# Down products of a macaron encoder layer: affine of tiles 0-3 two steps sooner, statistics of tiles 4-7 by a sum on VectorE and squares on ScalarE

## What is computed

```python
def sublayer(h, j, fn, resid_w):
    u = (_layer_norm(h) * (1.0 + scale) + shift).astype(h.dtype)
    z = DEEPNORM_ALPHA * h.astype(jnp.float32) + resid_w * gate * fn(u)
    return (_layer_norm(z) * ln_g[layer, j] + ln_b[layer, j]).astype(h.dtype)

def _layer_norm(x):
    mu = jnp.mean(xf, axis=-1, keepdims=True)
    var = jnp.mean(jnp.square(xf - mu), axis=-1, keepdims=True)
    return (xf - mu) * lax.rsqrt(var + LN_EPS)

def _swiglu(u, w_gate, w_up, w_down):
    return (jax.nn.silu(u @ w_gate) * (u @ w_up)) @ w_down
```

## Time and profile before

| | |
|---|---|
| time, median of 3 runs | 2078.71 us (2077.89 to 2082.67) |
| profiled execution | 2078.98 us, span 2077.2 us |
| TensorE busy | 1959.9 us (94%) |
| VectorE busy | 1195.8 us (58%) |
| ScalarE busy | 801.3 us (39%) |
| GpSimd busy | 606.4 us (29%) |
| TensorE waits, 1960 us to the end | 2.7 us for VectorE L1465, 2.0 for L1431 (extra), 0.7 for L1431 (4 times) |

### The profile page before, as it was taken

The page is one execution under the profiler, slowest core; times in us unless marked ns, Lnnn a source line. Parts: engine busy times, 40 slices in busy tenths (PEclk is TensorE's granted clock), DMA queues, the critical chain, the costliest instruction groups (busy, mean ns, idle before and its releaser), DMA issues. The chain is left out here.

```text
span 2077.2 us, 27306 instructions
## 1 busy us (share of the span) xinstructions
PE 1959.9 (94%) x9962; PEld 1532.6 (74%) x9962; DVE 1195.8 (58%) x2056; ACT 801.3 (39%) x1397; POOL 606.4 (29%) x433
## 2 busy tenths in 40 slices
PE   6899999999999969999889997889999999999996
PEld 4677777777888747777567775778788888887884
DVE  5855555555686963344424445587744444457778
ACT  4533333333445363343413434336433333334541
POOL 0353444333960010000041331001543443449300
PEclk9999999999999989999999999999999999999998
DMA  9255454555874323111042220612233323367732
GB/s 318 64 192 163 163 180 160 179 166 171 317 246 144 101 62 100 30 42 41 11 106 50 41 61 31 233 71 92 95 114 102 108 95 102 117 227 264 251 99 102
DMA packets 184885, 270.56 MB, mean 130 GB/s; under 512 B 12592, under 2 KB 111152, under 8 KB 184624
## 3 DMA queue, kind: packets, MB, share of 16 engines
q1 hardware_dynamic: 153888, 235.18, 33.8%
q10 hardware_dynamic: 29840, 29.50, 4.5%
q0 software_dynamic: 1024, 4.13, 1.2%
HBM read 210.84 MB, written 57.93 MB: 129 GB/s over the span
## 5 line engine op out<-in xcount | busy, mean ns | idle before, releaser
L1581 PE MATMUL f_ps<-f_uh,f_ops 128*128 128x512 f32 x2496 | 783.0, 392 | 13.1 <-DVE f_ops L1272 4.2
L1581 PEld LDWEIGHTS f_ps<-f_uh,f_ops 128*128 128x128 f32 x2496 | 469.6, 188 | 127.5 <-issue 24.1
L1581 PE MATMUL f_ps<-f_ul,f_ops 128*128 128x512 f32 x1248 | 487.6, 391 | 0.0
L966 POOL TENSOR_TENSOR f_sums<-f_raw 128x512 f32<-128x512 f32 x80 | 113.0, 1413 | 547.6 <-DVE f_ul L1401 238.0
L1581 PEld LDWEIGHTS f_ps<-f_ul,f_ops 128*128 128x128 f32 x1248 | 235.0, 188 | 47.6
L1431 DVE TENSOR_TENSOR f_dl<-f_blocks,f_dh 128x1024 fp32r<-128x1024 f32 (+1 forms) x146 | 202.4, 1401 | 81.5 <-ACT f_dh L1162 81.1
L1162 ACT CAST f_dh<-f_blocks 128x1024 fp32r<-128x1024 f32 (+1 forms) x146 | 144.3, 990 | 228.2 <-PE f_ps L1715 225.6
L1715 PE MATMUL f_ps<-f_dh 128*128 128x512 f32 x496 | 196.1, 395 | 9.3 <-DVE f_ev L1465 4.9
L1272 DVE TENSOR_TENSOR f_ops<-f_sums,f_ops 128x512 fp32r<-128x512 f32 x160 | 119.6, 748 | 139.8 <-ACT f_ops L1027 139.7
L1715 PE MATMUL f_ps<-f_dh,f_dl 128*128 128x512 f32 x496 | 194.7, 393 | 0.0
L1715 PE MATMUL f_ps<-f_dl,f_dh 128*128 128x512 f32 x496 | 194.7, 393 | 0.0
(11 more groups left out here) (249 smaller groups left out, 2987.3 us busy)
## 6 DMA issues: line engine op xcount, KB each, us to landing
f_hidden<-acc SPq DMA_DIRECT2D x154, 256.0 KB, 3.8
f_blocks<-f_hidden SPq DMA_DIRECT2D x154, 256.0 KB, 3.5
f_blocks<-in_ffn_w_down SPq DMA_DIRECT2D x132, 256.0 KB, 6.0
f_raw<-in_ffn_w_gate SPq DMA_DIRECT2D x20, 1024.0 KB, 6.1
f_raw<-in_ffn_w_up SPq DMA_DIRECT2D x20, 1024.0 KB, 5.3
f_aw<-in_w_ada ACTq DMA_DIRECT2D x28, 512.0 KB, 3.6
acc<-in_w_ada ACTq DMA_DIRECT2D x28, 512.0 KB, 4.7
in_raw<-in_w_in SPq DMA_DIRECT2D x24, 512.0 KB, 3.9
```

The costliest lines, as they stand in the source:

```text
L966: nc.gpsimd.tensor_tensor(sums[:, x], of, with_, how).then_inc(s_done, 1)
L1581: done = nc.tensor.matmul(ps[:, bank, :], l[:, k, :], r[:, k, :], start=fresh and k == 0 and m == 0, stop=closed and k == HK - 1 and m == ...
```

## The change

Three things are changed in `ffn_phase`, for both parts.

1. Tiles 0 to 3: ScalarE's root of the first pair is at step 61 and of the second at step 62 (both were at 62); VectorE's coefficients are at 61 and 62 (63), the affines at 62 to 65 (64 to 67).
2. Product 5: the weighing is done for two tiles behind low part 72 and for two behind the loop (was at 69), the residual behind the loop (was at 70). The bn_stats of tiles 4 to 7 are gone. The residual writes the row sum of its output into a small field instead (`accum_out`).
3. Tiles 4 to 7: ScalarE makes the mean out of the two sums, squares the tile's deviation from it with a sum (`last_deviation`), and takes the root. VectorE gates and adds the next tile first, and then makes the coefficients (four instructions) and the affine of the tile before. The squares' elements go to a scratch area over the weight blocks of product 6, which are free by then. In FFN 1 ScalarE's work for the mixer is ordered anew around these.

```diff
--- before.py
+++ after.py
@@ -607,6 +607,7 @@
         self.gates = m.at(tag + "_gates", [P, D], at_aw)
         self.ev = m.at(tag + "_ev", [P, 4, NB], at_h + 24 * BL)
         self.rows = m.at(tag + "_rows", [P, 2, D], at_h + 28 * BL)
+        self.squares = m.at(tag + "_squares", [P, 4, D], self.t2[0] * BL)
         if ada:
             nrm = m.at(tag + "_next_nrm", [P, TT, D], at_h + 8 * BL)
             self.next_nrm = [nrm[:, t, :] for t in range(TT)]
@@ -683,6 +684,8 @@
     t_out, c_out, d_mm, d_gated = sem("t_out"), sem("c_out"), sem("d_mm"), sem("d_gated")
     d_out, bc_ld = sem("d_out"), sem("bc_ld")
     shifted_v, gained_v = sem("shifted_v"), sem("gained_v")
+    l_half, l_mean, l_squared, l_std, l_small, l_coef = (sem(f"l_{x}") for x in ("half", "mean", "squared", "std", "small",
+                                                                                 "coef"))
     stored = sem("stored") if ent is None else ent.stored
     m_ld, m_turned, m_col = sem("m_ld"), sem("m_turned"), sem("m_col")
     AW = 256
@@ -695,7 +698,7 @@
         a_mm, a_part, a_row = sem("a_mm"), sem("a_part"), sem("a_row")
     with ExitStack() as st:
         ps = Parts(nc, st).ps(tag + "_ps", [P, 8, NB])
-        lv = Normaliser(nc, top, mem.small, tag + "_lv", ((0, 1), (2, 3), (4,), (5,), (6,), (7,)))
+        lv = Normaliser(nc, top, mem.small, tag + "_lv", ((0, 1), (2, 3)))
         block = st.enter_context(nc.Block())
         XB, YB, ZB = (0, 3), (1, 4), (2, 5)
         TURN = (6, 7, 2, 5)
@@ -1208,9 +1211,8 @@
                             copy_out(r, x, t)
                 if 0 <= n - 4 * KD - 1 < KD:
                     third_hi(n - 4 * KD - 1)
-                if n == 62:
-                    lv.root(act, 0)
-                    lv.root(act, 1)
+                if n in (61, 62):
+                    lv.root(act, n - 61)
                 if n == 64 and ent is not None:
                     act.wait_ge(m_turned, 1)
                     src = ps[:, Y_BANKS[0], 0:2 * 3 * KT].rearrange("p (j w k) -> p j w k", j=2, w=3)
@@ -1218,31 +1220,50 @@
                     for j in range(2):
                         nc.scalar.copy(dst[:, 1 + j, 0], src[:, j, 0]).then_inc(m_col, 1)
                         nc.scalar.activation(dst[:, 1 + j, 1], src[:, j, 1], ACT.Copy, bias=1.0).then_inc(m_col, 1)
+            def field(t, x):
+                return lv.sm[:, t, x:x + 1]
+
+            def last_deviation(t):
+
+                act.wait_ge(d_out, 9 + t)
+                nc.scalar.activation(field(t, 12), field(t, 0), ACT.Identity, bias=field(t, 2),
+                                     scale=1.0 / D).then_inc(l_mean, 1)
+                act.wait_ge(l_mean, t - 3)
+                nc.scalar.activation(mem.squares[:, t - 4, :], acc[:, t, :], ACT.Square, bias=field(t, 12), scale=-1.0,
+                                     accum_out=field(t, 13)).then_inc(l_squared, 1)
+                act.wait_ge(l_squared, t - 3)
+                nc.scalar.activation(field(t, 14), field(t, 13), ACT.Sqrt, bias=lv.eps[:, 0:1],
+                                     scale=1.0 / D).then_inc(l_std, 1)
+
             if ent is not None:
                 act.wait_ge(shifted_v, 4)
                 ent.mean(act, 0, 4, 1)
                 act.wait_ge(d_mm, steps_done(6 * KD - 1))
                 for t in range(4):
                     ent.square(act, t, acc[:, t, :])
-            lv.root(act, 2)
+                ent.root(act, 0, 4)
+            act.wait_ge(d_out, 12)
+            act.wait_ge(d_lo, ND)
+            nc.scalar.activation(lv.sm[:, 4:TT, 2], lv.sm[:, 4:TT, 1], ACT.Copy, scale=1.0 / D).then_inc(l_half, 1)
+            act.wait_ge(l_half, 1)
+            last_deviation(4)
             if ent is not None:
-                ent.root(act, 0, 4)
-            lv.root(act, 3)
+                for t in range(2):
+                    ent.normalise(act, t, acc[:, t, :], 1)
+            last_deviation(5)
             if ent is not None:
+                for t in range(2, 4):
+                    ent.normalise(act, t, acc[:, t, :], 1)
                 act.wait_ge(shifted_v, 5)
                 ent.mean(act, 4, 5, 2)
                 act.wait_ge(c_out, 12)
                 ent.square(act, 4, acc[:, 4, :])
-                for t in range(2):
-                    ent.normalise(act, t, acc[:, t, :], 1)
-            lv.root(act, 4)
+            last_deviation(6)
             if ent is not None:
-                for t in range(2, 4):
-                    ent.normalise(act, t, acc[:, t, :], 1)
                 act.wait_ge(shifted_v, 6)
                 ent.mean(act, 5, 6, 3)
                 ent.square(act, 5, acc[:, 5, :])
-            lv.root(act, 5)
+            last_deviation(7)
             if ent is not None:
                 act.wait_ge(shifted_v, 7)
                 ent.mean(act, 6, 7, 4)
@@ -1478,12 +1499,18 @@
                 half = 1 if r in (4, 5) else 0
                 of = acc[:, t if r < 5 else 4 + t, NB * half:NB * half + NB]
                 dve.wait_ge(d_gated, 4 * x + t + 1)
-                nc.vector.scalar_tensor_tensor(of, of, ALPHA, mem.ev[:, t, :], ALU.mult, ALU.add).then_inc(d_out, 1)
+                if r < 5:
+                    nc.vector.scalar_tensor_tensor(of, of, ALPHA, mem.ev[:, t, :], ALU.mult, ALU.add).then_inc(d_out, 1)
+                else:
+                    nc.vector.scalar_tensor_tensor(of, of, ALPHA, mem.ev[:, t, :], ALU.mult, ALU.add,
+                                                   lv.sm[:, 4 + t, 6 - r:7 - r]).then_inc(d_out, 1)
 
             def affine(t):
 
-                g = [t in x for x in lv.groups].index(True)
-                dve.wait_ge(lv.coef_done, g + 1)
+                if t < 4:
+                    dve.wait_ge(lv.coef_done, t // 2 + 1)
+                else:
+                    dve.wait_ge(l_coef, t - 3)
                 mean, r = lv.sm[:, t, 12:13], lv.sm[:, t, 18:19]
                 w = D // parts_of(t)
                 for i in range(parts_of(t)):
@@ -1506,11 +1533,14 @@
                     if n == KD * (r + 1) + 2:
                         for t in range(4):
                             add_up(r, t)
-                    if n == KD * (r + 1) + 3:
+                    if r < 5 and n == KD * (r + 1) + 3:
                         if r == 1:
                             dve.wait_ge(g_half, 1)
                         for t in range(4):
                             weigh(r, t)
+                if n == ND - LAST + DRING - 1:
+                    for t in range(2):
+                        weigh(5, t)
                 if 0 <= n - 4 * KD - 1 < KD:
                     third_lo(n - 4 * KD - 1)
                 if n in (36, 37):
@@ -1533,32 +1563,45 @@
                         dve.wait_ge(d_out, 4 + t + 1)
                         lv.half(dve, acc[:, t, :], t, 1)
                         lv.both(t)
-                if n == 63:
-                    lv.coefficients(dve, 0)
-                    lv.coefficients(dve, 1)
+                if n in (61, 62):
+                    lv.coefficients(dve, n - 61)
+                if n == 62:
                     dve.wait_ge(bc_ld, 32)
-                if 64 <= n < 68:
-                    affine(n - 64)
-                if n == 70:
-                    for t in range(4):
-                        dve.wait_ge(h_ld[4 + t], 16)
-                        residual(5, t)
-                if n == 71:
-                    for t in range(4):
-                        dve.wait_ge(d_out, 8 + t + 1)
-                        lv.half(dve, acc[:, 4 + t, :], 4 + t, 1)
+                if 62 <= n < 66:
+                    affine(n - 62)
+            for t in range(2, 4):
+                weigh(5, t)
+            for t in range(4):
+                dve.wait_ge(h_ld[4 + t], 16)
+                residual(5, t)
+
+            def last_coefficients(t):
+
+                squares, std, inv, a_, b_, r = (lv.sm[:, t, x:x + 1] for x in range(13, 19))
+                dve.wait_ge(l_std, t - 3)
+
+                def chained(n, ins):
+                    ins.then_inc(l_small, 1)
+                    dve.wait_ge(l_small, 3 * (t - 4) + n)
+
+                chained(1, nc.vector.reciprocal(inv, std))
+                chained(2, nc.vector.scalar_tensor_tensor(a_, squares, D * EPS, inv, ALU.add, ALU.mult))
+                chained(3, nc.vector.scalar_tensor_tensor(b_, a_, -0.5 / D, inv, ALU.mult, ALU.mult))
+                nc.vector.scalar_tensor_tensor(r, b_, 1.5, inv, ALU.add, ALU.mult).then_inc(l_coef, 1)
+
+            dve.wait_ge(d_out, 12)
             for t in range(4, TT):
                 dve.wait_ge(d_mm, tile_done(6, t - 4))
                 nc.vector.tensor_tensor(mem.ev[:, t - 4, :], ps[:, bank(6, t - 4), :], mem.gates[:, 0:NB],
                                         ALU.mult).then_inc(d_gated, 1)
                 residual(6, t - 4)
-                dve.wait_ge(d_out, 8 + t + 1)
-                lv.half(dve, acc[:, t, :], t, 0)
-                lv.both(t)
```

(9 more changed lines are left out.)

## The result

| | before | changed |
|---|---|---|
| median | 2079.44 us (4 runs, 2077.89 to 2082.67; the 2078.71 above is that of three of them) | 2062.26 us (4 runs, 2060.78 to 2062.71) |
| profiled execution | 2078.98, span 2077.2 | 2060.78, span 2059.0 |

The ratio is 0.9913 with a 95% interval of 0.9901 to 0.9925, so 17.2 us faster in the medians and 18.2 in the spans. A second measurement of the same two kernels gave 0.9904 (0.9887 to 0.9920), 19.2 us in the medians. The forecast was 2060.7 us, range 2057.5 to 2067.

A forecast was written before the change was run, and what follows sets the result against it. TensorE is busiest, so VectorE and ScalarE changes pay only where TensorE waits or has ended. Gains of 8.6 us (FFN 2) and 9.4 (FFN 1), together 18.0, give 2061.0 profiled, 2060.7 as median; range 2057.5 to 2067.

The forecast's parts named there:

- Part 1: Ahead of step 66: early affine restarts TensorE 2.1 us sooner in FFN 2, leaving a pause of 0.6.
- Part 2: Steps 69 to 76: moved VectorE work leaves TensorE no second pause; tile 4's product comes 7.8 us sooner in FFN 2.
- Part 3: Tiles 4 to 7: VectorE needs 4.9 us per tile instead of 6.37, under TensorE's 5.45; the residual's sum costs 0.
- Where I said the parts meet: Tiles 4 to 7: TensorE becomes the pace; VectorE takes tile 4 up 1.8 us late, made good before tile 5.
- Sum: Both feed-forward parts: gains of 8.6 us in FFN 2 and 9.4 in FFN 1, together 18.0.
- Rival A: Behind the pause left ahead of step 66, TensorE's clock still falls: 1.8 us per part, 2064.3; chance 0.12.
- Rival B: FFN 1's tail: late normalisations and deviations in ScalarE's queue make VectorE wait, 8 us in all, 2069; chance 0.08.
- least slack 1.4: FFN 1's tail: ScalarE's deviations are ready at least 1.4 us before they are wanted; lateness costs beyond that.
- C: ScalarE in tiles 4 to 7: table loads of 1.28 us between Identity, Square and Sqrt, 2065 to 2068; chance 0.05.
- D: From step 66 on: the clock falls for the whole tails, up to 42 us slower; chance 0.03.
- E: Before step 66: early affine makes low parts late, so no gain shows; 0.06 including gains under 6.2 us otherwise caused.

The follow-up runs named there:

- e4: The changed kernel with product 5's weighing in one lot at 69 and the residual at 70; 2.7 and 2.8 us longer, span 2064.7, ratio 0.9939.
- e2: The changed kernel with the early roots and affine of tiles 0 to 3 undone; 1.9 and 3.9 us longer, span 2066.1, ratio 0.9947.
- e3: The kernel before with early affine and moved weighing and residual, but bn_stats kept instead of sums; 3.1 and 3.4 us shorter, ratio 0.9974.
- e1: The kernel before with only the early roots and affine of tiles 0 to 3; 1.3 and 1.2 us shorter, ratio 0.9978.
- e11: The changed kernel itself, measured again beside the kernel before; span 2060.8 us, ratio 0.9904.
- e10: The changed kernel with five more half-width VectorE operations ahead of product 5's sums, pause 4.00 us; 6.1 and 6.6 us longer, span 2074.0.
- e5: The changed kernel with the squares of tiles 4 to 7 taken twice on ScalarE; FFN 1 1.9 us longer, FFN 2 0.0, span 2063.3.
- e7: The changed kernel with product 5's sums behind low part 67 instead of 68; 0.6 to 0.7 us shorter per part, ratio 0.9909.

## Why the prediction was right, step by step

- **Part 1.** Predicted: TensorE resumes 3.3 us after high part 68 starts in FFN 2 and 3.0 in FFN 1; measured 3.06 and 3.05. I had VectorE last by 0.2; it was ScalarE's high part 68, by 0.34 in FFN 2 and 0.73 in FFN 1. In FFN 2 VectorE took 0.6 less than I had added up: I priced four half-width low parts at their duration of 0.68 and not at the 0.60 from start to start, and the two coefficient chains at 0.97 where they took 0.82 and 0.88. The pause left is 0.37, not 0.6. The table load was hidden, as said.
- **Part 2.** No second pause, low part 76 ends 15.0 behind the start of high part 68 (15.2 predicted), tile 7's product 30.2 behind the restart (30.2 predicted). e4 shows what the two lots and the later residual are worth: 2.7 and 2.8 per part, all of it TensorE's.
- **Part 3.** VectorE's work behind the last product: 8.3 and 8.1 measured, 8.4 and 8.1 predicted. The residual's sum costs nothing: L1505 starts every 0.61 us with it, as it did before without. The prediction had priced a rule of the Trainium skill's page "Vector Engine (DVE) Microarchitecture Reference", section "Points that are easy to get wrong", at 0.6 for the sum. That did not come: if the halved throughput that the page names is there, it is there with and without the sum. The rows:

```profile
2030.10 0.68 DVE L1505 SCALAR_TENSOR_TENSOR acc<-acc,f_ev 128x512 f32<-128x512 f32 x1
2030.71 0.08 DVE L1505 DVE_READ_ACCUMULATOR acc<-acc,f_ev 128x1 f32 x1
2030.71 0.68 DVE L1505 SCALAR_TENSOR_TENSOR acc<-acc,f_ev 128x512 f32<-128x512 f32 x1
```

- **Where I said the parts meet.** Once TensorE is the pace, what it loses or gains arrives at the end in full: e2's pause and clock, 1.9 and 3.9. By the ruler parts 1 and 2 give 6.5 (e3), parts 2 and 3 give 12.4 (e2), parts 1 and 3 give 12.7 (e4), and all together 18.3. So taken out of the whole, part 1 is worth 5.8, part 2 5.5 and part 3 11.8, more than 18.3 together: the parts do not simply add, each is worth more beside the others. Part 1 alone gave 2.5 (e1).
- **Sum.** 18.0 predicted, 18.3 by the ruler, 18.2 in the spans; 17.2 in the medians, whose interval (0.9901 to 0.9925) holds it. By part 9.4 were predicted in FFN 1 and 9.4 measured, 8.6 in FFN 2 and 8.9 measured; of those 0.3, 0.2 is the earlier restart and 0.1 the work behind the last product. The forecast of 2060.7 lies 1.6 under the first median and 0.1 over that of e11. That it is so close has some luck in it: it starts from an execution in which the clock fell behind the first pause in both parts, and e2 shows that in FFN 1 it need not.
- **Rival A, the clock.** Right that 0.4 us does nothing; the price of 1.8 was about right where it came (1.6 in e2's FFN 2) and nought in e2's FFN 1. The rival's picture, one pause and its length, is too simple: the fall in the mixer comes behind shorter pauses. What the page "TensorE: Matmul & The Clock Gate" of the Trainium skill says in its section "HAM oscillation — how this bites in real kernels", that long idle gaps bring the clock down, agrees with e10, where both pauses of 4.00 did. The gaps of which that section speaks are longer than the 1.89, 2.27 and 2.67 us behind which the clock fell here, and there the measurement decides.
- **Rival B, ScalarE's queue.** It did not come, but my reason for its small chance was wrong in one step: I read "least slack 1.4" as if each tile had its own. That 1.4 comes from FFN 2's times (3.4 less 2.0; measured 1.42 at tile 7). In the times listed for FFN 1 the least slack is 1.9, at tile 7, and it measured 1.29. e5 took 1.2 per tile and lost 1.9 in FFN 1, where by that reading it should have lost nothing. The forecast held because the real work fitted, not because there was room for 1.4 more.
- **Rivals C, D and E.** No table load in either tail behind the first root's, no slow matmul in either tail, and no low part late before step 66. For C the prediction names rows 9, and there are no rows of that number; what shows that Sqrt, Identity and Square follow one another without a load is ScalarE's timeline in FFN 1 of the kernel before (L157 is the root, L242 an Identity, L211 a square):

```profile
728.43 0.29 ACT L157 ACTIVATE f_lv_sm<-f_lv_sm,f_lv_eps 128x1 f32<-128x1 f32 x1
728.64 2.36 ACT L242 ACTIVATE f_next_nrm<-acc,f_next_sm 128x1024 f32<-128x1024 f32 x2
...
731.12 1.15 ACT L211 ACTIVATE f_next_nrm<-acc,f_next_sm 128x1024 f32<-128x1024 f32 x1
```

## What to carry to other kernels

Follow one restart through: which instruction releases the engine, what it needs next, and who is the pace from there; in the traces the early affine alone gave 2.5 us, and 5.8 beside the rest of the change. Price a queue from start to start, and price slack over the whole stretch in which an engine never idles, not per item. For effects under 0.1% find a stretch in the traces that starts and ends on events of the same work: it showed 0.65 us per part twice, where medians showed nothing. But where the clock can fall, one trace is one execution: set it beside the times of the others, as e1 shows.

## What the hardware showed beside

- An idle time of 0.37 us in the profile was 0.65 us of lost time (e7): the profile counts from the modelled end of the last matmul (0.39 long, while the next starts 0.23 after it), and the first matmul behind the pause took 0.47 with its successor 0.31 later. Together that is 0.37 + 0.16 + 0.08 = 0.61. A short pause cost more here than its bracket says.
- The same pause of 2.27 us at the same place was followed by a clock of about half in one execution and by full clock in another (before, e2).
